# A hybrid decoder layer on one core: the steps of each mixing tile put at other places in the program of the projection and of the feed-forward part

## The chip, the cores and the metric

One core of one Trainium2 chip runs the whole layer in one launch. The metric is device microseconds of a run. The kernel before takes 2847.31 us (median of three runs, 2841.47 to 2847.5). Five engines matter here: TensorE (PE, with its weight loads PEld), VectorE (DVE), ScalarE (ACT), GpSimd (POOL, unused) and SyncE (SP), which issues nearly all DMAs. Each runs its own list of instructions in order; between engines there are only semaphores.

## The reference, cut to what matters

2048 tokens of width 1024 in float32 go through one layer:

```
z   = rms_norm(x) @ w_in                       # 1024 -> 2560
rwkv  = delta-rule recurrence on token-shifted z[:, :1792], 8 heads x 64, then group norm and gate
swa   = windowed softmax attention (128 tokens, sinks, relative bias) on z[:, 1792:], 8 query heads, 2 kv heads
x   = x + concat(rwkv, swa) @ w_out
x   = x + square(relu(rms_norm(x) @ w_ff_up)) @ w_ff_down      # 1024 -> 4096 -> 1024
x   = x + rms_norm(p @ ple_proj) * sigmoid(x @ ple_gate)
out = rms_norm(x)
```

The recurrence is computed in chunks of 64 tokens: decays by a cumulative sum, scores inside a chunk, a triangular inverse built by doubling, and a state of 64x64 per head that is carried from chunk to chunk.

## The kernel before, in words

**Large matrix products.** Tokens come in 4 blocks of 512. Every float32 operand of a large product is split into a rounded part (`hi`, made by ACT) and the rest (`lo`, made by DVE), and three products are added: hi by hi, hi by lo, lo by hi. Weights come in chunks of 128x1024; a chunk is used for 24 matmuls of 128x512. Its `w_hi` is a copy on ACT (line 991), its `w_lo` a subtraction on DVE (line 1312). There are two buffers of each, so chunk n+1 is prepared while PE uses chunk n.

**Two programs side by side.** The work is written as generators that `yield`. The *fill* is the large products: `proj` (projection of a block, lines 583 to 587) or `fin` (output projection, feed-forward, gate: lines 829 to 833 and 871 to 875). Between two yields of the fill PE has, with few exceptions, half a chunk, 12 matmuls; this is called a piece here. The other program is `mix`: the recurrence and the attention of one tile of 128 tokens, 16 tiles in all, each cut into 27 steps (0 to 26). `side_by_side` merges them: a table gives for each step of four tiles a *place*, the number of pieces of the fill that come ahead of it. All engines follow the same table, each with its own part of the step.

- `BESIDE_PROJ`: tiles 0 to 3 beside the projection of blocks 1 to 3 (128 pieces). Pieces 1 to 44 are block 1, 45 to 88 block 2, 89 to 128 block 3. The first 14 of a block's 20 chunks also give DVE the token shift of the projected rows (lines 1356 to 1365) between its two halves.
- `BESIDE_FIN`: tiles 4 to 7 beside `fin` of block 0, and by the same table 8 to 11 and 12 to 15 beside blocks 1 and 2. The fourth `fin` runs alone.

**What the steps do on PE**, and what they wait for:

| step | PE | waits for |
|---|---|---|
| 0 | nothing, but it waits | `rw` of the tile before (DVE, step 25, line 1583) |
| 1 | lora and gate products (640 to 644) | sigmoid of ACT, step 0 (1090) |
| 2 | norms (651) | ACT sigmoids of step 1 (1097) |
| 4 | spread (658) | ACT square root, DVE reciprocal, ACT copy (1101, 1448, 1104) |
| 6 | bonus and transposes (665, 628) | DVE steps 4 and 5 (1459 to 1473) |
| 8, 9 | scores (685), then av and logits (697 to 605) | DVE and ACT copies, DVE masks |
| 10 to 14 | doubling levels (713); probabilities turned (614) at 12; values (622) at 13 | DVE `m` of the level (1514); DVE probabilities (1411) |
| 15, 16 | inverse blocks (728, 735), turn (614) | DVE inverse (1529), DVE copy |
| 17 | values (622), u and w (748, 754) | ACT copy of the turned probabilities (1084), DVE copy |
| 18, 19 | state applied (762), state grown (770, 771), first chunk | DVE copies `wT` (1552), `sa` (1415) |
| 20, 21 | the same, second chunk, and output parts (792, 794) | DVE `state0` (1425), `sa` (1415) |
| 22 | output from the state (802) | itself |
| 25 | output transposed (810) | DVE `y_norm` (1578), after mean and variance in steps 22 to 24 |

Within a step's place nothing of the fill lies between two steps: if steps 18 and 19 have one place, PE waits for the copy between them; if they are one piece apart, it has 12 large matmuls to do in that time. DVE and ACT have the same order: a DVE operation of a step that has to wait holds back the `w_lo` behind it.

Of the kernel before, what the change touches and what calls it, by code (L numbers as in the profile page):

```python
# [161 lines left out]
for _turned, _last in (("turn0", "out1_3"), ("xt0", "ple1_3")):  # L162
# [15 lines left out]
FIN_CHUNKS = 8 + HG * 16 + 2 + 8  # L178


BESIDE_PROJ = (3, 5, 5, 5, 6, 7, 9, 11, 13, 14, 15, 17, 19, 20, 22, 24, 26, 27, 27, 28, 29, 29, 29, 29, 29, 31, 31, 31, 34, 34, 34, 35,
# [3 lines left out]
BESIDE_FIN = (0, 1, 2, 4, 4, 4, 6, 6, 10, 12, 13, 16, 18, 22, 23, 25, 28, 29, 31, 32, 33, 34, 34, 35, 38, 38, 40, 40, 40, 44, 46, 46,  # L185
# [3 lines left out]


def side_by_side(fill, tiles, places):


    assert len(places) == MIX_STEPS * len(tiles)
    given = 0
    for i, place in enumerate(places):
        while given < place:
            next(fill)
            given += 1
        next(tiles[i // MIX_STEPS])  # L200
    for t in tiles:
        assert next(t, None) is None
    for _ in fill:
        pass


def one_after_another(*parts):
    for p in parts:
        yield from p


def whole_program(norm, proj, mix, fin):

    for part in (norm(0), proj(0)):
        for _ in part:
            pass
    side_by_side(one_after_another(proj(1), proj(2), proj(3)), [mix(t) for t in range(TPB)], BESIDE_PROJ)
    for b in range(1, BLOCKS):
        side_by_side(fin(b - 1), [mix(t) for t in range(b * TPB, (b + 1) * TPB)], BESIDE_FIN)
    for _ in fin(BLOCKS - 1):  # L220
# [1559 lines left out]
```

## Time and profile before

| | |
|---|---|
| runs | 2847.31 us median, 2841.47 to 2847.5 (3 runs) |
| profiled execution, span | 2842.6 us; 4.7 us under the median |
| PE busy | 2784.0 us (98%) |
| DVE, ACT busy | 1737.4 us (61%), 1167.5 us (41%) |
| DMA | 317.47 MB, 112 GB/s |
| projection beside tiles 0 to 3 | 134 to 616 us |
| `fin` of blocks 0, 1, 2 beside tiles | 616 to 1200, to 1783, to 2367 us |
| `fin` of block 3 alone | 2367 to 2842.6 us |

The trace gives the span; the times of whole runs include what lies around it. The page puts an operation's idle time in front of it and names what ended the wait. A PE matmul here lasts 0.39 us by the record but the next starts 0.23 us after it, since matmuls overlap; so the distance between starts is what counts, and a stop under 0.16 us isn't seen as idle time.

### The profile page before, as it was taken

What the parts mean: (1) busy time and instruction counts of PE and PEld (TensorE: products, weight loads), DVE (VectorE), ACT (ScalarE), POOL (GpSimd) and SP (SyncE); (2) the same over time, 40 slices, a digit from 0 to 9 for tenths busy, and PEclk for the clock granted to TensorE, in tenths of its full rate; (3) what the DMA queues carried; (4) which work ended last, traced back from release to release, by engine and by line L of the source; (5) the groups of instructions that cost most, each with busy time, mean ns of one, the idle gap of its engine ahead of it and who ended that gap; (6) DMA issues with size and microseconds to landing.
All of it is one profiled execution on the core that took longest, in us unless ns stands there. A gap on an engine that the chain in (4) does not pass through costs nothing.

```text
span 2842.6 us, 54416 instructions
## 1 busy us (share of the span) xinstructions
PE 2784.0 (98%) x23651; PEld 2251.3 (79%) x23651; DVE 1737.4 (61%) x2886; ACT 1167.5 (41%) x1942; POOL 0.2 (0%) x4
## 2 busy tenths in 40 slices
PE   8999999999999999999999999999999999999998
PEld 6877777777878787878887777878887788888876
DVE  5476676756666565675756566766575655443335
ACT  4354344344433342564333334543343335332225
POOL 0000000000000000000000000000000000000000
PEclk9999999999999999999999999999999999999999
DMA  6553443453333232343332333423333225233332
GB/s 211 162 167 97 146 130 97 136 178 98 89 95 95 86 96 93 122 157 91 92 93 85 96 96 130 155 75 92 101 95 87 84 96 185 89 96 97 97 101 77
DMA packets 369738, 317.47 MB, mean 112 GB/s; under 512 B 47291, under 2 KB 322012, under 8 KB 369500
## 3 DMA queue, kind: packets, MB, share of 16 engines
q1 hardware_dynamic: 365104, 309.58, 35.7%
q10 hardware_dynamic: 4396, 4.41, 0.5%
q8 instruction: 187, 3.06, 0.4%
q14 instruction: 51, 0.42, 0.0%
HBM read 276.18 MB, written 39.32 MB: 111 GB/s over the span
## 4 chain that ended last, share of the span: by engine, by line
PE 78%; DVE 2%; DMA 1%; ACT 1%; issue 0%; SPq 0%; ACTq 0%
PE ps L829 13%; PE ps L833 12%; PE ps L832 12%; PE ps L871 9%; PE ps L875 8%; PE ps L874 8%; PE ps L713 1%; PE ps L583 1%; PE ps L586 1%; PE ps L587 1%; PE ps L605 1%; DMA wraw_f<-in_w_gate 1%; PE ps L614 1%; PE ps L622 1%; PE ps L685 1%; PE ps L628 1%
## 5 line engine op out<-in xcount | busy, mean ns | idle before, releaser
L1312 DVE TENSOR_TENSOR w_lo<-wraw_f,w_hi 128x1024 fp32r<-128x1024 f32 x408 | 498.8, 1222 | 405.4 <-ACT w_hi L991 404.5
L991 ACT ACTIVATE w_hi<-wraw_f 128x1024 fp32r<-128x1024 f32 x408 | 430.9, 1056 | 553.4 <-PE ps L829 462.8
L829 PE MATMUL ps<-w_hi,h_hi 128*128 128x512 f32 x1280 | 513.0, 401 | 7.2 <-DVE rw L1583 4.4
L833 PE MATMUL ps<-w_hi,h_lo 128*128 128x512 f32 x1280 | 499.6, 390 | 0.0
L832 PE MATMUL ps<-w_lo,h_hi 128*128 128x512 f32 x1280 | 498.8, 390 | 0.0
L871 PE MATMUL ps<-act_hi,w_hi 128*128 128x512 f32 x1024 | 408.4, 399 | 0.4
L875 PE MATMUL ps<-act_hi,w_lo 128*128 128x512 f32 x1024 | 399.3, 390 | 0.0
L874 PE MATMUL ps<-act_lo,w_hi 128*128 128x512 f32 x1024 | 398.9, 390 | 0.0
L829 PEld LDWEIGHTS ps<-w_hi,h_hi 128*128 128x128 f32 x1280 | 240.3, 188 | 62.8 <-issue 7.9
L833 PEld LDWEIGHTS ps<-w_hi,h_lo 128*128 128x128 f32 x1280 | 240.2, 188 | 52.3
L832 PEld LDWEIGHTS ps<-w_lo,h_hi 128*128 128x128 f32 x1280 | 240.7, 188 | 46.4
L1192 ACT ACTIVATE h_hi<-tmp 128x512 fp32r<-128x512 f32 x128 | 80.9, 632 | 405.7 <-DVE tmp L1634 405.7
L871 PEld LDWEIGHTS ps<-act_hi,w_hi 128*128 128x128 f32 x1024 | 192.2, 188 | 43.5 <-issue 3.7
L875 PEld LDWEIGHTS ps<-act_hi,w_lo 128*128 128x128 f32 x1024 | 192.2, 188 | 41.2
L874 PEld LDWEIGHTS ps<-act_lo,w_hi 128*128 128x128 f32 x1024 | 192.4, 188 | 37.5
L1637 DVE TENSOR_TENSOR h_lo<-tmp,h_hi 128x512 fp32r<-128x512 f32 x128 | 88.7, 693 | 159.5 <-ACT tmp L1193 159.5
L1634 DVE SCALAR_TENSOR_TENSOR tmp<-ps,stage_f 128x512 f32<-128x512 f32 x128 | 88.2, 689 | 117.5 <-PE ps L875 114.8
L583 PE MATMUL ps<-act_hi,w_hi 128*128 128x512 f32 x320 | 129.9, 406 | 5.5 <-DVE rw L1583 2.9
L583 PE MATMUL ps<-h_hi,w_hi 128*128 128x512 f32 x320 | 129.2, 404 | 2.8 <-DVE rw L1583 1.5
L829 PE MATMUL ps<-w_hi,act_hi 128*128 128x512 f32 x320 | 127.4, 398 | 2.7 <-DVE w_lo L1312 2.3
L587 PE MATMUL ps<-act_hi,w_lo 128*128 128x512 f32 x320 | 125.8, 393 | 0.0
L586 PE MATMUL ps<-act_lo,w_hi 128*128 128x512 f32 x320 | 125.8, 393 | 0.0
(231 smaller groups left out, 4078.8 us busy)
## 6 DMA issues: line engine op xcount, KB each, us to landing
wraw_f<-in_w_ff_up SPq DMA_DIRECT2D x256, 256.0 KB, 3.3
wraw_f<-in_w_ff_down SPq DMA_DIRECT2D x128, 512.0 KB, 4.0
wraw_f<-in_w_in SPq DMA_DIRECT2D x80, 512.0 KB, 4.3
zT<-tmp SPq DMA_DIRECT2D x80, 256.0 KB, 2.1
wraw_f<-in_w_out SPq DMA_DIRECT2D x32, 512.0 KB, 4.0
wraw_f<-in_w_gate SPq DMA_DIRECT2D x32, 512.0 KB, 5.1
zs<-zT SPq DMA_DIRECT2D x16, 896.0 KB, 6.6
h_lo<-mixT SPq DMA_DIRECT2D x4, 2048.0 KB, 8.1
```

What stands on the lines that cost most here:

```text
L583: mm = T.matmul(dst, wh, hi[:, k, :], start=(k == 0), stop=False)
L586: T.matmul(dst, wh, lo[:, k, :], start=False, stop=False)
L587: mm = T.matmul(dst, wl, hi[:, k, :], start=False, stop=(k == DK - 1))
L829: mm = T.matmul(ps[:, j, :], ah, wh, start=(first and k == 0), stop=False)
L832: T.matmul(ps[:, j, :], ah, wl, start=False, stop=False)
L833: mm = T.matmul(ps[:, j, :], al, wh, start=False, stop=(final and k == 1))
L871: mm = T.matmul(ps[:, bank, :], wh, act_hi[:, k, :], start=(k == 0), stop=False)
L874: T.matmul(ps[:, bank, :], wh, act_lo[:, k, :], start=False, stop=False)
L875: mm = T.matmul(ps[:, bank, :], wl, act_hi[:, k, :], start=False, stop=(k == DK - 1))
L991: S.activation(w_hi[:, n % 2, :], raw[:, n % 4, :], ACT.Copy).then_inc(w_hi_done, 1)
L1312: V.tensor_tensor(w_lo[:, n % 2, :], raw[:, n % 4, :], w_hi[:, n % 2, :].bitcast(F32), ALU.subtract).then_inc(w_lo_done, 1)
L1637: V.tensor_tensor(h_lo[:, i, :], tmp[:, i % 2, :], h_hi[:, i, :].bitcast(F32), ALU.subtract).then_inc(fin_dve.mark(f"h_lo{g}_{i}"), 1)
```

## The change: other places for the steps, in both tables

Only the numbers of the two tables change. Every instruction is the same, and so is the fill. One line of each table:

```diff
-BESIDE_PROJ = (3, 5, 5, 5, 6, 7, 9, 11, 13, 14, 15, 17, 19, 20, 22, 24, 26, 27, 27, 28, 29, 29, 29, 29, 29, 31, 31, 31, 34, 34, 34, 35,
+BESIDE_PROJ = (11, 14, 15, 19, 21, 24, 26, 26, 30, 34, 35, 37, 39, 40, 42, 43, 45, 46, 47, 48, 50, 52, 52, 55, 55, 59, 61, 61, 62,
...
-BESIDE_FIN = (0, 1, 2, 4, 4, 4, 6, 6, 10, 12, 13, 16, 18, 22, 23, 25, 28, 29, 31, 32, 33, 34, 34, 35, 38, 38, 40, 40, 40, 44, 46, 46,
+BESIDE_FIN = (0, 1, 2, 4, 4, 4, 6, 6, 8, 12, 13, 14, 15, 19, 23, 25, 28, 29, 30, 32, 34, 36, 37, 37, 38, 41, 41, 42, 43, 44, 45, 46,
```

Places of the steps that matter, before and after (tile 0 is the first of a table's four):

| table, tile | steps | before | after |
|---|---|---|---|
| projection, 0 | 0, 1, 2, 4 | 3, 5, 5, 6 | 11, 14, 15, 21 |
| projection, 0 | 17 to 22; 25; next 0 | 27, 27, 28, 29, 29, 29; 31; 31 | 46, 47, 48, 50, 52, 52; 59; 61 |
| projection, 1 | 0, 1, 2, 4, 5 | 31, 34, 34, 35, 35 | 61, 62, 62, 62, 62 |
| projection, 1 | 13, 14, 15, 16 | 49, 50, 53, 54 | 75, 75, 76, 78 |
| projection, 1 | 17 to 22; 25; next 0 | 55, 55, 55, 55, 56, 56; 61; 61 | 78, 78, 78, 78, 78, 78; 81; 81 |
| projection, 2 | 1, 2, 4 | 63, 63, 64 | 83, 83, 84 |
| projection, 2 | 17 to 22; 25; next 0 | 84, 84, 84, 85, 85, 85; 87; 88 | 98, 98, 98, 98, 98, 98; 100; 101 |
| projection, 3 | 0, 1, 2, 4, 5 | 88, 89, 89, 90, 92 | 101, 102, 102, 102, 102 |
| projection, 3 | 13, 14, 15 | 106, 107, 109 | 113, 113, 114 |
| projection, 3 | 17 to 22; 25 | 112, 113, 113, 114, 115, 115; 119 | 117, 117, 117, 117, 117, 117; 119 |
| fin, 0 | 10, 11, 12, 13 | 13, 16, 18, 22 | 13, 14, 15, 19 |
| fin, 2 | 24, 25; tile 3: 0, 1 | 110, 113; 113, 115 | 109, 111; 112, 112 |
| fin, 3 | 24, 25, 26 | 153, 158, 158 | 153, 158, 158 |

Tile 0 beside the projection gets 50 pieces instead of 28, the other three get some 20 each instead of 27 to 31. Beside `fin` every tile keeps about its share.

PE beside the projection, second tile, norms and spread (names: `ones` and `work` into `ps` are the norms, `alpha_t` the spread; `w_hi`, `w_lo` and `act` are the fill). Before:

```order
L641 MATMUL ps<-zs,lora 128x128
L644 MATMUL ps<-zs,gup 128x128 x4
L651 MATMUL ps<-ones,work 128x2 [waits mix_act]
L651 MATMUL ps<-ones,work 128x2 x3
L583 MATMUL ps<-act_hi,w_hi 128x512
L586 MATMUL ps<-act_lo,w_hi 128x512
L587 MATMUL ps<-act_hi,w_lo 128x512
```

The same place after:

```order
L641 MATMUL ps<-zs,lora 128x128
L644 MATMUL ps<-zs,gup 128x128 x4
L651 MATMUL ps<-ones,work 128x2 [waits mix_act]
L651 MATMUL ps<-ones,work 128x2 x3
L658 MATMUL ps<-con,alpha_t 128x128 [waits mix_act]
L658 MATMUL ps<-con,alpha_t 128x128 x3
L583 MATMUL ps<-h_hi,w_hi 128x512 [waits proj_act,w_lo_done]
```

The piece of the fill that lay between norms and spread has gone behind the spread.

DVE beside the projection, third tile, its end (`work<-ps` at 1552 is `wT`, at 1415 `sa`; `state`, then the sums of `y`). Before:

```order
L1552 COPY work<-ps 128x2x4x64 [waits mix_pe]
L1415 COPY work<-ps 64x2x4x64 [waits mix_pe]
L1420 TENSOR_TENSOR small<-ps,state 128x256 [waits mix_pe]
L1425 TENSOR_TENSOR state<-small,ends 128x256 [waits mix_dve]
L1312 TENSOR_TENSOR w_lo<-wraw_f,w_hi 128x1024 [waits w_hi_done]
L1415 COPY work<-ps 64x2x4x64 [waits mix_pe]
L1420 TENSOR_TENSOR small<-ps,state 128x256 [waits mix_pe]
L1425 TENSOR_TENSOR state<-small,ends 128x256 [waits mix_pe,mix_dve]
```

After:

```order
L1552 COPY work<-ps 128x2x4x64 [waits mix_pe]
L1415 COPY work<-ps 64x2x4x64 [waits mix_pe]
L1420 TENSOR_TENSOR small<-ps,state 128x256 [waits mix_pe]
L1425 TENSOR_TENSOR state<-small,ends 128x256 [waits mix_dve]
L1415 COPY work<-ps 64x2x4x64 [waits mix_pe]
L1420 TENSOR_TENSOR small<-ps,state 128x256 [waits mix_pe]
L1425 TENSOR_TENSOR state<-small,ends 128x256 [waits mix_pe,mix_dve]
```

The weight chunk's `w_lo` no longer lies between the two halves; steps 17 to 22 are one run of waits.

PE beside `fin`, end of the third tile (810 is the transposed output, 829 to 833 the fill, `lora` the first product of the fourth tile). Before:

```order
L833 MATMUL ps<-w_hi,h_lo 128x512
L810 MATMUL ps<-con,work 128x128 [waits mix_dve]
L810 MATMUL ps<-con,work 128x128 x3
L829 MATMUL ps<-w_hi,h_hi 128x512 [waits mix_dve]
L832 MATMUL ps<-w_lo,h_hi 128x512
```

After:

```order
L810 MATMUL ps<-con,work 128x128 [waits mix_dve]
L810 MATMUL ps<-con,work 128x128 x3
L829 MATMUL ps<-w_hi,h_hi 128x512
L832 MATMUL ps<-w_lo,h_hi 128x512
...
L833 MATMUL ps<-w_hi,h_lo 128x512
L640 MATMUL ps<-zs,lora 128x128 [waits mix_act,mix_dve]
L641 MATMUL ps<-zs,lora 128x128
```

The wait for `rw` stands one piece later, ahead of the next tile's first product.

## Rows read from the trace of the kernel before

**Rows 1.** Windows by stage; columns: stretch, length, busy by engine, PEclk, DMA.
```profile
134.00:616.00 482.00, 463.62 (x4861) 371.74 (x4860) 330.61 (x648) 204.83 (x358) 0.00 (x0) 0.99 0.45 134
616.00:1200.00 584.00, 577.26 (x5387) 464.68 (x5386) 370.08 (x612) 243.45 (x409) 0.00 (x0) 1.00 0.33 101
```
**Rows 2.** PE's waits, 134 to 616 us: total, times, longest.
```profile
PE ps L583 <- DVE rw L1583: 4.4, 2, 2.9
PE ps L770 <- DVE work L1415: 3.9, 5, 0.8
PE ps L583 <- DVE w_lo L1312: 3.1, 3, 1.4
PE ps L762 <- DVE work L1552: 2.4, 3, 0.8
PE ps L640 <- ACT zs L1090: 1.5, 2, 1.2
PE ps L651 <- ACT work L1097: 1.3, 4, 0.7
PE ps L762 <- DVE state L1425: 1.0, 1, 1.0
```
**Rows 3.** PE's waits, 616 to 2358 us.
```profile
PE ps L829 <- DVE rw L1583: 4.4, 3, 1.5
PE ps L640 <- ACT zs L1090: 3.1, 1, 3.1
PE ps L614 <- DVE work L1411: 2.3, 3, 0.8
```
**Rows 4.** Timeline of PE: start, us, what, idle before.
```profile
253.37 0.63 PE L586 MATMUL ps<-act_lo,w_hi 128*128 128x512 f32 x1
253.80 0.63 PE L587 MATMUL ps<-act_hi,w_lo 128*128 128x512 f32 x1
...
399.94 0.39 PE L586 MATMUL ps<-h_lo,w_hi 128*128 128x512 f32 x1
400.17 0.40 PE L587 MATMUL ps<-h_hi,w_lo 128*128 128x512 f32 x1
...
675.78 1.04 PE L842 MATMUL ps<-con,x 128*128 128x128 f32 x8
```
**Rows 5.** Windows at the two falls of the granted clock.
```profile
248.50:251.90 3.40, 1.38 (x9) 0.93 (x7) 3.27 (x8) 3.35 (x4) 0.00 (x0) 1.00 0.22 73
344.00:351.00 7.00, 6.03 (x48) 4.88 (x44) 2.52 (x6) 0.00 (x0) 0.00 (x0) 0.51 0.01 2
```
**Rows 6.** Timeline, second tile, norms to spread and on.
```profile
264.53 1.05 PE L651 MATMUL ps<-ones,work 128*128 128x2 f32 x8 [0.16 <-ACT work L1097]
265.53 1.28 ACT L1101 ACT_TABLE_LOAD   x1
266.82 0.18 ACT L1101 ACTIVATE knorm<-ps 128x8 f32<-128x8 f32 x1
267.48 0.63 ACT L1104 ACTIVATE alpha_t<-knorm 128x512 f32<-128x512 f32 x1 [0.48 <-DVE knorm L1448]
273.51 0.69 DVE L1473 TENSOR_TENSOR work<-work 128x512 f32<-128x512 f32 x1
```
**Rows 7.** Timeline, second tile, steps 18 to 20 at one place.
```profile
341.98 0.68 PE L762 MATMUL ps<-state,work 64*64 64x64 f32 x16 [0.79 <-DVE work L1552]
345.96 1.12 PE L762 MATMUL ps<-state,work 64*64 64x64 f32 x16 [0.97 <-DVE state L1425]
347.01 0.79 PE L583 MATMUL ps<-h_hi,w_hi 128*128 128x512 f32 x1
```
**Rows 8.** Timeline, second tile, the copy that step 17 waits for.
```profile
335.83 1.03 ACT L1084 ACTIVATE work<-ps 128x1024 f32<-128x1024 f32 x1 [1.04 <-PE ps L614]
```
**Rows 9.** DVE groups by line: busy us, mean ns, idle before.
```profile
L1388 DVE SCALAR_TENSOR_TENSOR work<-ps,bias 128x512 f32<-128x512 f32 x64 | 40.7, 676 | 17.6 <-PE ps L605 17.2
L1396 DVE TENSOR_REDUCE top<-work 128x4 f32<-128x1024 f32 x32 | 39.0, 1220 | 1.1
```

12 rows, old and new, of tables (BESIDE_FIN, BESIDE_PROJ) are left out of this document.

## The prediction

> **What bounds the kernel now.** I read first the windows by stage: beside the projection TensorE (PE) is busy 463.6 of 482 us, beside a block of `fin` 577.3 of 584 [rows 1]. PE is the bound nearly everywhere, its work isn't changed, and other places can only move PE's stops. So next its waits: about 18 us beside the projection [rows 2] and about 10 us beside three blocks of `fin` [rows 3]. That is all there is to win. Third the timeline of PE: a large matmul follows the last by 0.23 us, a piece of twelve takes 12 x 0.228 = 2.73 us; after the longest stop beside the projection, 2.9 us, the same matmuls start 0.43 us apart [rows 2, 4]. Fourth the granted clock: the stretch ahead of the end of that stop had PE busy 1.38 of 3.40 us at full clock, then it fell to half (1.2 GHz); around 344 to 351 us it was at 0.51 [rows 5]. A stop is thus paid twice if the clock falls on it.
>
> Durations are from the profiled execution, whose span of 2842.6 us is 4.7 us under the median of the runs. I sum changes against its span and add them to the median, 2847.3; that gap is itself within the spread of the runs, so 0.2% (5.7 us) is what I count as no change.
>
> **Beside `fin`: what goes.** (a) The tile at places 75 to 113 ends with its transposes at 113, and the next tile's step 0, at 113 too, makes PE wait for `rw`: 4.4 us in three blocks [rows 3]. Now the transposes stand at 111, step 0 at 112, and its wait lands ahead of the lora product, one piece (2.73 us) later: longer than the 1.5 us waited. Nothing is left of it. (b) Level 2 with the turn of the probabilities stood at 18, behind a short piece of transposes, 1.04 us [rows 4], and with VectorE's (DVE's) `out_add` ahead of its DVE part: 2.3 us of waiting in three blocks, 0.8 each [rows 3]. Now it is at 15 behind a full piece of 2.73 us, 1.7 us more cover than before. Gone, but the DVE part of step 12 now comes ahead of the `out_add` that the first transposes wait for; I put 0.3 us a block, bounds 0 and 0.8 (the whole wait come back, by its row). Together with 0.1 us at each restart: -4.4 - 2.3 - 0.4 + 0.9 = **-6.2 us**; bounds -7.1 and -4.7. The first block's 3.1 us for ACT's sigmoid [rows 3] stays, since steps 0 and 1 keep 0 and 1 and the last steps of the table are the same. Everywhere else in this table dependent steps that come closer are one piece apart, as other tiles had them before without a stop.
>
> **Beside the projection: what goes.** Tile 0 gets room. The `rw` wait of 2.9 us at its end goes (25 at 59, next 0 at 61). Steps 0 to 5 go apart, so one `w_lo` wait of 1.4 us (of 3.1 in three) goes with the sigmoid's 0.3 and 0.5 us at the norms; its steps 20 and 21 part (0.8). Tile 3's sigmoid wait of 1.2 us goes, because at 101 ScalarE (ACT) comes to step 0 after preparing a chunk and not after a copy that needs the end of a piece, and so does the `w_lo` wait of 1.3 us behind it [rows 2]. Sum 2.9 + 1.4 + 1.3 + 1.5 + 0.5 + 0.8 = **-8.4 us**; bounds -6 and -9. Tile 1's `rw` wait of 1.5 us stays (25 and 0 both at 81).
>
> **What comes.** Tiles 1 to 3 get 20 pieces each and several dependent steps at one place.
> (c) Steps 2 and 4 at one place, in tiles 1 and 3. From the start of the norms to the end of ACT's copy is 264.53 to 267.48 + 0.63 = 268.11, 3.6 us; PE's own burst in it is 1.05 [rows 6]. The piece that covered this is gone: 2.6 us of waiting, twice, **+5.2**. DVE's part of steps 2 to 5 ends 274.20 - 264.53 = 9.7 us after the norms' start in both orders [rows 6], and the next `w_lo` then has until two pieces and the burst of step 6 are done (about 11.8 us), so no further stop: bounds 0 and 1.4 us a time, the latter the `w_lo` row.
> (d) Steps 17 to 22 at one place in tiles 1, 2 and 3. Each meeting is priced in this trace: 17 to 18 0.8 us, 18 to 19 and 20 to 21 0.8, 19 to 20 1.0 [rows 2, 7]. Before, 3, 5 and 1 of them met (7.4 us); after, 3, 6 and 3 (2.4 + 4.8 + 3.0 = 10.2). One of the 0.8 is counted in tile 0 already, so +2.8 + 0.8 = **+3.6**.
> (e) Tile 1 has step 17 at 78 with 16: ACT's copy of the turned probabilities, 1.03 us [rows 8], lies open, **+1.0**.
> (f) In tiles 1 and 3 steps 13 and 14 share a place and 15 is one piece later. DVE has the logits (2 x 0.68 + 1.22 us [rows 9]) and more ahead of the inverse. An estimate of 0.7 us each, bounds 0 and 2.6 (all of that work open), **+1.4**.
> (g) Tile 2 ends in a zone where DVE has the token shift, steps 22, 25, 0 at 98, 100, 101: 0.8 us for `y_norm` and `rw`, and 0.2 for the masks at 88: **+1.0**, bounds 0 and 2.9 (the `rw` wait of tile 0, which lay in such a zone).
> Without the clock the projection part is -8.4 + 5.2 + 3.6 + 1.0 + 1.4 + 1.0 = **+3.8 us**.
>
> **The clock.** Before it fell twice. After the 2.9 us stop a piece ran at 0.43 for 0.23 us [rows 4]: 12 x 0.20 = 2.4 us. In the run of steps 17 to 20 of tile 1 the second state product took 1.12 for 0.68 us [rows 7], and nine large matmuls after it 0.2 us more each: about 2.5 with the small ones. So 4.9 us were lost. After, the first cause is gone, but steps 17 to 22 make three runs that are each longer than that one. I take one fall in each: 3 x 2.5 = 7.5, **+2.6 us**. Bounds: none (-4.9) and five, with the two waits of (c) (+7.6). For (c) the row of the 2.9 us wait speaks for a fall, that of the 3.1 us wait at the start of `fin` against: there the stage ran at 1.00 [rows 1, 3].
>
> The Trainium skill, "TensorE: Matmul & The Clock Gate", section "HAM oscillation — how this bites in real kernels", says that waits which break up the stream of matmuls let the gate fall back to half rate, and that each later burst then starts cold. The half-rate matmuls after the 2.9 us wait agree [rows 4]; the 3.1 us wait didn't bring one. This is the rule that speaks most against the change, and it is weighed as the rival "slower" below.
>
> Sum: -6.2 + 3.8 + 2.6 = +0.2 us. Forecast **2848 us**, no change that can be told.
>
> **Rivals.** *Faster, 2837 us:* the three dense runs keep full clock, as the denser half of tile 2's end did before (17 to 19 at one place, no fall), and the estimates of (f) and (g) don't come: +0.2 - 7.5 - 2.4 = -9.7. For it: three of four tile ends of before had no fall inside them. Against: the one that had four steps at one place had it.
> *Slower, 2855 us:* the spread wait of (c) is where it is decided. DVE has 9.7 us of work in one place while the token shift of the fill waits behind it; if its `w_lo` comes late, PE stops again, 1.3 us twice, and the two waits together pull the clock down, 2.5 us twice: +0.2 + 7.6 = +7.8. It decides from the point where the clock falls at both. For it: such waits for `w_lo` followed the dense starts of tiles 0 and 3 [rows 2]. Against: the sum in (c), and the other `rw` wait, 1.5 us, brought no fall.
> *The waits beside `fin` only change their name, 2852 us:* the fourth tile's steps 0 and 1 now share place 112, and PE may wait there for the sigmoid, up to the 1.2 us of the projection [rows 2], three times: +0.2 + 3.6 = +3.8. Against it: the second tile had 40 and 40 there before and didn't stop.
> *Table switches of ACT cost twice in the open, 2850 us.* In the uncovered chain of (c) a table load stands, 1.28 us, and the square root starts at once behind it [rows 6]; if ACT held each of the two chains for that length once more, it is +2.6. Against it is the same row, which has nothing between load and square root.
> The Trainium skill, "ScalarE: Activation LUTs", section "What ACT_TABLE_LOAD costs", gives 1283 ns for the load and 1380 ns more for a drain at each switch. By it the chain in (c) would be 1.38 us longer each time, 2.8 us in all. The row has the load's 1.28 us and no drain behind it [rows 6], so the trace doesn't agree.
>
> **How the numbers follow.** Forecast 0.48, faster 0.20, slower 0.22, renamed waits 0.06, table switches 0.04. The forecast's own spread, from the bounds of (f), (g) and one fall more or less, is 2842 to 2854, a little of it beyond 0.2% on each side (0.03 faster, 0.04 slower). Faster: 0.19 of the faster case plus 0.03, 0.22; slower: 0.20 of the slower case plus 0.04, 0.24; the rest, 0.54, is no change. The range runs to both main rivals, 2837 to 2857; beyond it lie the cases in which all bounds fall to one side.
>
> **What would show it.** PE's waits beside `fin` for `rw` and for the probabilities are gone (6.7 us to under 1). Beside the projection PE waits for ACT's `alpha_t` copy ahead of line 658 twice, some 2.6 us each; six waits at line 770 and three for `state`; no wait of 2.9 us for `rw`. The granted clock falls three times, at the ends of tiles 1, 2 and 3. Stage by stage: projection +6 us, each `fin` block -2. The prediction is wrong if the clock falls not at all or five times, or if `w_lo` heads the waits beside the projection.

## The result: slower by 0.44%, and the profile after

The changed kernel takes 2856.22 us (median of five runs, 2854.35 to 2858.99), the kernel before 2842.13 us beside it; the ratio is 1.0044, 95% interval 1.0031 to 1.0057. That is slower by 12.5 us by the ratio, more than the 0.2% that I counted as no change. The time lies at the upper end of the range; the likeliest case, no change, didn't come true, and the rival "slower, 2855 us" did.

That the time lies so near to that rival's is in part luck. The prediction counted from 2847.3 us, the median of the first three runs of the kernel before; with two more runs that median is 2842.13. So the rival's change was +7.8 us and the range ended at +9.7 us, while the measured change is +12.5 us (8.8 to 16.2 by the interval): larger than either.

The page after, its first line and part 1 (busy us, share, instructions):

```profile
span 2854.2 us, 54416 instructions
PE 2794.3 (98%) x23651; PEld 2260.1 (79%) x23651; DVE 1740.3 (61%) x2886; ACT 1166.4 (41%) x1942; POOL 0.2 (0%) x4
```

The span is 11.6 us longer. The windows of the changed kernel, cut at the same matmul of the fill in each kernel (stretch, length, busy time by engine, PEclk, DMA): the projection beside tiles 0 to 3, its block 3 alone, and `fin` of block 1:

```profile
134.37:626.55 492.18, 469.05 (x4862) 379.40 (x4861) 331.57 (x648) 204.85 (x357) 0.00 (x0) 0.97 0.44 131
448.07:626.55 178.48, 167.74 (x2005) 135.52 (x2004) 118.68 (x232) 62.83 (x113) 0.00 (x0) 0.93 0.42 125
1214.71:1797.78 583.07, 580.76 (x5402) 466.84 (x5401) 379.21 (x628) 247.48 (x421) 0.00 (x0) 1.00 0.34 104
```

The same cuts in the kernel before:

```profile
133.48:615.76 482.28, 463.90 (x4862) 371.97 (x4861) 330.61 (x648) 205.12 (x357) 0.00 (x0) 0.99 0.45 134
1203.02:1786.87 583.85, 580.33 (x5401) 467.34 (x5400) 378.53 (x628) 247.66 (x421) 0.00 (x0) 1.00 0.34 104
```

The projection is 9.9 us longer; the two full `fin` blocks are 0.8 and 0.9 us shorter. The rest of the 11.6 us: 0.9 us more ahead of the projection and 1.6 us in `fin` 3, whose programs are as before, and 0.9 us in `fin` 0. Each of the three has a stretch at half clock (6.8, 3.4 and 3.4 us) that the trace of the kernel before has not. PE's waits beside the projection (total, times, longest), against [rows 2]:

```profile
PE ps L658 <- ACT alpha_t L1104: 5.3, 2, 2.8
PE ps L770 <- DVE work L1415: 4.8, 6, 0.8
PE ps L762 <- DVE state L1425: 2.9, 3, 1.0
PE ps L583 <- DVE w_lo L1312: 2.6, 2, 2.0
PE ps L762 <- DVE work L1552: 2.4, 3, 0.8
PE ps L728 <- DVE work L1529: 1.5, 2, 0.8
PE ps L553 <- DVE rw L1583: 1.5, 1, 1.5
PE ps L622 <- ACT work L1084: 1.2, 1, 1.2
```

All of PE's waits there add up to 22.9 us instead of 18.1 (the windows above give 23.1 and 18.4). Beside `fin`, against [rows 3]:

```profile
PE ps L640 <- ACT zs L1090: 3.1, 1, 3.1
PE ps L829 <- DVE w_lo L1312: 2.3, 3, 0.8
PE ps L829 <- DVE act_lo L1643: 1.8, 3, 0.6
PE ps L871 <- DVE w_lo L1312: 1.4, 3, 0.5
PE ps L842 <- DVE act_lo L1622: 0.8, 3, 0.3
```

The waits for `rw` and for the probabilities are gone, and three smaller ones stand there, the last three rows (the first two rows were there before). Now the clock. It was at half beside the projection in five stretches, four of them below (the fifth, 3.4 us, from 336 us on):

```profile
401.00:407.70 6.70, 4.92 (x90) 4.55 (x88) 1.97 (x4) 0.00 (x0) 0.00 (x0) 0.50 0.05 9
493.20:499.90 6.70, 5.98 (x116) 5.79 (x120) 1.04 (x2) 0.00 (x0) 0.00 (x0) 0.50 0.26 41
517.10:523.80 6.70, 5.10 (x14) 4.22 (x15) 6.15 (x16) 5.25 (x9) 0.00 (x0) 0.50 0.26 78
585.30:595.50 10.20, 8.37 (x148) 7.80 (x148) 1.97 (x4) 0.00 (x0) 0.00 (x0) 0.50 0.17 27
```

401, 493 and 585 us are the ends of tiles 1, 2 and 3 (steps 17 to 22 at one place); 336 and 517 us are the two waits of the spread. 34.1 us at half clock in all, against 13.7 before. The first wait of the spread, on PE's timeline, against [rows 6]:

```profile
332.55 1.05 PE L651 MATMUL ps<-ones,work 128*128 128x2 f32 x8 [0.15 <-ACT work L1097]
336.17 1.12 PE L658 MATMUL ps<-con,alpha_t 128*128 128x128 f32 x4 [2.57 <-ACT alpha_t L1104]
```

From the start of the norms to the spread is 3.62 us, as it was when a piece lay over it, and the spread itself ran at half clock (1.12 us for four transposes that take 0.60 at full).

This is one execution of each kernel, and the clock isn't the same in every one. e2 and e7 below have the old table beside the projection, so this stage is the same program in them as in the kernel before. Their windows, e2 first:

```profile
133.74:613.46 479.72, 461.36 (x4863) 370.12 (x4861) 330.61 (x648) 204.88 (x357) 0.00 (x0) 0.99 0.46 135
133.84:612.46 478.62, 460.12 (x4862) 368.98 (x4861) 330.64 (x648) 204.90 (x357) 0.00 (x0) 1.00 0.46 135
```

PE stands idle 18.4 and 18.5 us in them, as before, but the half clock lasts 6.8 and 3.4 us instead of 13.7, and the stage is 2.6 and 3.7 us shorter: about 0.37 us for each us at half clock. The new program of the stage (the changed kernel and e1) ran twice too, with 34.1 and 41.0 us at half clock, in 492.2 and 497.2 us. So some us of a stage's length belong to the execution and not to the table.

### The profile page after: what moved, and what is told of

Read it like the earlier page. It is cut to its first block, busy times and chain, and to the rows that moved or that the text cites. A ratio compares the mean times of both kernels' runs of the same rounds, so it can differ in the third digit from the quotient of the medians.

```text
span 2854.2 us, 54416 instructions
## 1 busy us (share of the span) xinstructions
PE 2794.3 (98%) x23651; PEld 2260.1 (79%) x23651; DVE 1740.3 (61%) x2886; ACT 1166.4 (41%) x1942; POOL 0.2 (0%) x4
## 4 chain that ended last, share of the span: by engine, by line
PE 76%; DVE 3%; ACT 2%; DMA 1%; issue 1%; SPq 0%; ACTq 0%
PE ps L829 12%; PE ps L833 12%; PE ps L832 12%; PE ps L871 9%; PE ps L875 8%; PE ps L874 8%; PE ps L713 1%; PE ps L605 1%; DMA wraw_f<-in_w_gate 1%; PE ps L622 1%; PE ps L583 1%; PE ps L614 1%; PE ps L586 1%; PE ps L587 1%; PE ps L685 1%; PE ps L770 1%
## 5 line engine op out<-in xcount | busy, mean ns | idle before, releaser
L875 PE MATMUL ps<-act_hi,w_lo 128*128 128x512 f32 x1024 | 399.2, 390 | 0.0
L874 PE MATMUL ps<-act_lo,w_hi 128*128 128x512 f32 x1024 | 399.0, 390 | 0.0
L586 PE MATMUL ps<-h_lo,w_hi 128*128 128x512 f32 x320 | 125.9, 393 | 0.0
L587 PE MATMUL ps<-h_hi,w_lo 128*128 128x512 f32 x320 | 125.8, 393 | 0.0
```

The source lines that it names most:

```text
L586: T.matmul(dst, wh, lo[:, k, :], start=False, stop=False)
L587: mm = T.matmul(dst, wl, hi[:, k, :], start=False, stop=(k == DK - 1))
L874: T.matmul(ps[:, bank, :], wh, act_lo[:, k, :], start=False, stop=False)
L875: mm = T.matmul(ps[:, bank, :], wl, act_hi[:, k, :], start=False, stop=(k == DK - 1))
```

## Experiments

Four readings were open at first. **A**: the loss is made beside the projection, by steps that meet at one place and by the falls of the clock that these meetings bring. Rivals: **B**, the `fin` table has a good part in it; **C**, the waits count and the falls cost next to nothing; **D**, VectorE is behind in the dense tiles whatever the order, so that a wait taken away turns up as another. In the kernels e1 to e4 the lines stand 6 lower than in the listing (line 652 is 658 there), in e6 6 to 10 higher, since the tables or the code ahead have another length.

### e1 and e2: one table each

```diff
 e1: the new BESIDE_PROJ, the old BESIDE_FIN
 e2: the old BESIDE_PROJ, the new BESIDE_FIN
```

> The new table beside the projection alone, the old one beside fin. Theory A (the loss is made beside the projection, by steps that meet at one place and by the falls of the clock that this brings): the projection stage is 10 us longer than before, as in the changed kernel, the fin blocks as before; about 2852 to 2855 us, ratio 1.004. Rival B (the fin table has a good part in it): 2845 us, ratio 1.001.

Measured 2859.5 us, ratio 1.0055 (1.0041 to 1.0069): more than A had. In the trace the projection stage is 14.9 us longer than before and not 10, with 41.0 us at half clock and 24.7 us of idle time.

> The new table beside fin alone, the old one beside the projection. Theory A: 0.8 us less in each of three blocks, 2840 us, ratio 0.999; the waits for rw and for the probabilities are gone, and new ones of 0.5 us for w_lo, 0.3 us for act_lo and 0.6 us for the split of p stand in their place. My prediction's own size for it was 2 us a block, 2836 us. Rival B: slower than before, 2846 us or more.

Measured 2844.39 us, ratio 0.9997 (0.9988 to 1.0005); `fin` of blocks 1 and 2 583.2 and 583.5 us. All of the loss comes with the table beside the projection. B falls. By the trace the `fin` table is worth 0.7 us a block, a third of what I had put; the whole times can't show so little.

### e3 and e5: the spread behind a piece again

```diff
 e3: tiles 1 and 3 beside the projection, steps 2, 4, 5, 6
-62, 62, 62, 64 and 102, 102, 102, 104
+62, 63, 63, 64 and 102, 103, 103, 104
```

> The changed kernel with steps 4 and 5 one piece later in tiles 1 and 3 beside the projection (62 to 63, 102 to 103), nothing else. Theory A: the two waits of 2.6 and 2.7 us at line 658 go, and with them the two falls of the clock there: 8 to 10 us less than the changed kernel, about 2847 us. Rival C (waits alone count, the falls cost next to nothing): 5 us less, 2851 us. Rival D (VectorE is behind there anyway, so the wait moves to w_lo): within 1 us of the changed kernel.

Measured 2863.81 us, ratio 1.0070 (1.0057 to 1.0083): slower than the changed kernel, which none of the three had. PE's waits beside the projection in e3 (first two):

```profile
PE ps L659 <- DVE work L1464: 10.8, 2, 5.5
PE ps L764 <- DVE work L1409: 4.7, 6, 0.8
```

The waits of 2.6 us are gone, and line 659 (665 in the listing, step 6) waits 5.4 us twice for step 5. The first of the two, on the timelines of ScalarE and VectorE:

```profile
339.82 1.04 ACT L985 ACTIVATE w_hi<-wraw_f 128x1024 fp32r<-128x1024 f32 x1
340.89 1.22 DVE L1306 TENSOR_TENSOR w_lo<-wraw_f,w_hi 128x1024 fp32r<-128x1024 f32 x1 [2.85 <-ACT w_hi L985]
344.56 1.13 DVE L1464 SCALAR_TENSOR_TENSOR work<-work,par,zs 128x128 f32<-128x128 f32 x4
```

With the piece between steps 2 and 4, the next `w_lo` stands ahead of step 5 on VectorE. It needs `w_hi`, and ScalarE starts that only at 339.82 us, behind a table load and three activations of the tile (2.9 us). So VectorE stands idle for 2.85 us, a time in which it began step 5 in the changed kernel, and then `w_lo` and 3.7 us of step 5 follow, with one piece on PE to cover them. It is the same at tile 3, 2.85 us again. I had moved the wait one step on and made it larger. So e5 moved what hangs on it too:

```diff
 e5: the same tiles, steps 4 to 9
-62, 62, 64, 64, 66, 68 and 102, 102, 104, 105, 106, 107
+63, 63, 65, 65, 67, 69 and 103, 103, 105, 106, 107, 108
```

> The changed kernel with steps 4 and 5 one piece later in tiles 1 and 3 beside the projection, and now steps 6 to 9 too (63, 63, 65, 65, 67, 69 and 103, 103, 105, 106, 107, 108), so that VectorE has two pieces for step 5 as in the kernel before. Theory A: no wait at line 658 and none at 665; the two falls of the clock at the spread go; 2847 to 2850 us. Rival D (VectorE is behind in these places whatever the order): waits of 2 us or more at 665 or for w_lo stay, 2854 us or more.

Measured 2858.38 us, ratio 1.0058 (1.0045 to 1.0070), not told apart from the changed kernel's. Three of its waits:

```profile
PE ps L583 <- DVE w_lo L1312: 6.9, 4, 2.7
PE ps L685 <- DVE kappa_t L1488: 1.4, 1, 1.4
PE ps L665 <- DVE work L1470: 1.3, 2, 0.7
```

The falls at the spreads didn't come (23.9 us at half clock), but the idle time grew to 25.4 us, with `w_lo` at its head. What D foretold came: the wait turned up elsewhere, and the time is over 2854 us. But D's reason, VectorE's own amount of work, isn't what the trace shows. Here too VectorE stands idle 2.85 us ahead of that `w_lo`, until ScalarE has done its share of the tile's start and then `w_hi`; PE waits 1.7 us for this `w_lo` in tile 1 and 1.8 us in tile 3. So the tile's start is held by the chain of ScalarE's tile work, `w_hi` and `w_lo`. Whether a `w_hi` put ahead of that tile work would cure it was not tried.

### e4: one piece inside the tile's end

```diff
 e4: steps 16, 17 to 19, 20 to 22 of tiles 1, 2, 3 beside the projection
-78, 78, 78; 97, 98, 98; 116, 117, 117
+78, 78, 79; 96, 97, 98; 115, 116, 117
```

> The changed kernel with one piece of the fill put between steps 19 and 20 of tiles 1, 2 and 3 beside the projection, nothing else but what this pushes (tile 2 and 3 have steps 16 to 19 one piece earlier, tile 1 steps 20 to 24 one later). Theory A: the three waits of 1.0 us at line 762 for the state go, and the runs of small matmuls are short enough that the clock falls in at most one of the three: 3 us by the waits and 4 to 7 us by the clock, about 2847 us. Rival C (waits alone): 3 us less, 2853 us, with the falls in place or without cost.

Measured 2850.15 us, ratio 1.0027 (1.0016 to 1.0038): 4.8 us less than the changed kernel by the two ratios. The time lies between the forecasts of A (2847) and C (2853), and the intervals of the two ratios overlap, so the trace has to decide. The waits for the state are gone, while the wait for `sa` (line 764, 770 in the listing) grew in one place:

```profile
PE ps L764 <- DVE work L1409: 6.3, 6, 2.4
PE ps L652 <- ACT alpha_t L1098: 5.3, 2, 2.8
```

Idle time as a whole is even 0.8 us more (23.7 for 22.9), so the waits explain none of the gain. Time at half clock fell from 34.1 to 17.1 us, and the projection stage is 2.8 us shorter in spite of the idle time: some 3.6 us for 17.0, 0.2 us for each us at half clock. This speaks for A and against C. A's count was off, though: the clock still fell in four of the five places, two of them tile ends (1 and 3), for 3.4 us each time, and once more for 3.4 us at 160 us.

### e6: the waits kept, and filled

```diff
+def busy(n, tiles=(2, 3)):
+    if t in tiles:
+        for _ in range(n):
+            T.matmul(ps[:, 3, :], act_hi[:, 0, 0:P], act_hi[:, 0, :], start=True, stop=True)
 # behind the norms of tile 3: busy(11); behind steps 17, 18, 19, 20 of tiles 2 and 3: busy(4) each
```

> The changed kernel with matmuls that nobody reads (128x512, 0.23 us each, into a bank that is free in block 3 of the projection) in the waits of tiles 2 and 3: eleven behind the norms of tile 3, four behind each of steps 17, 18, 19 and 20 of tiles 2 and 3. The waits keep their length and are filled. Theory A (half of the loss is the clock): the three falls at 493, 517 and 585 us don't come, 24 us at half clock are gone, and it is 6 to 9 us faster than the changed kernel, 2847 to 2850 us, though it does more work. Rival C (only the waits cost): within 1 us of the changed kernel, or up to 1 us slower by the fillers that outlast a wait.

Measured 2853.27 us, ratio 1.0038 (1.0025 to 1.0051). The windows of e6: block 3 of the projection, and the three places where the clock had fallen:

```profile
451.31:623.25 171.94, 170.54 (x2048) 135.02 (x2047) 118.56 (x232) 62.85 (x113) 0.00 (x0) 1.00 0.44 130
480.00:500.00 20.00, 20.00 (x292) 15.60 (x292) 10.95 (x22) 3.56 (x5) 0.00 (x0) 1.00 0.33 100
500.00:530.00 30.00, 29.42 (x210) 23.44 (x207) 24.95 (x55) 19.43 (x31) 0.00 (x0) 1.00 0.33 90
575.00:600.00 25.00, 24.94 (x367) 20.04 (x362) 13.08 (x25) 5.89 (x8) 0.00 (x0) 1.00 0.29 75
```

With 43 more matmuls block 3 took 171.94 us instead of 178.48: 6.5 us less, at full clock all through. The waits were as long as before (the norms of tile 3 to its spread 3.80 us, for 3.82); only the 23.9 us at half clock are gone. That gives 6.5 / 23.9 = 0.27 us lost for each us at half clock, 1.9 us for a fall of 6.8 us. C falls for this block. The whole gained less than its block, 1.7 us by the ratios, where A had 6 to 9, and the intervals overlap: the whole times alone wouldn't decide. In this execution the blocks ahead, which have no fillers, took 3.4 us more than in the changed kernel's: the fall at tile 1 lasted 10.2 us instead of 6.8, and there was one more of 3.4 us at 160 us.

### e7, e9 and e10: what the fin table gives and takes

```diff
 e7: the kernel before, fin, tile 0: steps 11, 12; tile 2: steps 24, 25, 26
-16, 18; 110, 113, 113
+14, 15; 110, 111, 112
 e9:  as e2, tile 0 step 13:  19 -> 22
 e10: as e2, tile 3 steps 3 to 10:  117, 123, 125, 128, 129, 133, 136, 136 -> 117, 120, 123, 125, 125, 128, 133, 134
```

> The kernel before with only two places of the fin table changed in kind: tile 0 steps 11 and 12 at 14 and 15 (was 16, 18), tile 2 steps 25 and 26 at 111 (was 113). Theory E (the new fin table cures the two waits of 0.8 and 1.5 us a block and pays it back by three new ones that come from its other changes): without those, 2.3 to 2.5 us a block, 7 us in all, ratio 0.9975, 2836 us. Rival F (the two waits come back elsewhere whatever the rest does): 2841 us or more.

Measured 2839.66 us, ratio 0.9987 (0.9978 to 0.9996). By the traces `fin` 1 is 581.96 us, 1.9 us less than before, and so are the others; 5.8 us in three blocks, of which the medians show 3.7. That is between E (2836 us) and F (2841 us or more); the blocks speak for E, whose 2.3 to 2.5 us a block were somewhat too many. (Step 26 of tile 2 stood at 112, not at 111.) Its waits beside `fin` are these, without the first block's for the sigmoid:

```profile
PE ps L829 <- DVE w_lo L1312: 2.3, 3, 0.8
PE ps L842 <- DVE act_lo L1622: 0.8, 3, 0.3
```

> The fin-only kernel (old table beside the projection, new one beside fin) with step 13 of tile 0 back at 22 (was 19). Read from the waits, since the times are too close. Theory E: the wait of 0.5 us for w_lo at line 871 at the first chunk of the feed-forward part goes in all three blocks, since VectorE no longer has the second logits (4.4 us) ahead of that w_lo; the 0.3 us for act_lo at 842 stays, as it comes from steps 11 and 12 being early. Rival: both stay or both go.

> The fin-only kernel with steps 3 to 10 of tile 3 back at 117 to 134. Theory E: the wait of 0.6 us at line 829 for act_lo of line 1643 (the split of p, piece 133) falls back to the 0.1 us of before, since the four masks of step 8 (2.7 us of VectorE) no longer stand at 133 ahead of it; the others stay. Rival: 0.5 us or more stays.

Both were run once (2842.95 and 2843.07 us); only their waits are read. e9:

```profile
PE ps L829 <- DVE w_lo L1312: 2.4, 3, 0.8
PE ps L829 <- DVE act_lo L1643: 1.8, 3, 0.6
PE ps L842 <- DVE act_lo L1622: 0.8, 3, 0.3
```

and e10:

```profile
PE ps L829 <- DVE w_lo L1312: 2.3, 3, 0.8
PE ps L871 <- DVE w_lo L1312: 1.4, 3, 0.5
PE ps L842 <- DVE act_lo L1622: 0.8, 3, 0.3
```

Each took away the wait that was named and left the other. The three new waits have three causes: step 13 (VectorE's logits ahead of a `w_lo`), step 8 of tile 3 (its masks ahead of the split of p; e10 moved steps 4 to 10 together), and, as the wait that e7, e9 and e10 all keep, steps 11 and 12 (ahead of the `out_add`). No run undid the last one alone.

### e11: the meeting of norms and spread alone, in the roomy table

```diff
 e11: the kernel before, tiles 1 and 3 beside the projection, steps 2, 4, 5
-34, 35, 35 and 89, 90, 92
+34, 34, 34 and 89, 89, 89
```

> The kernel before with steps 4 and 5 put at the place of step 2 in tiles 1 and 3 beside the projection (34 and 89), nothing else. It prices the uncovered spread by itself in the roomy table. Theory A: two waits of 2.6 us at line 658, and a fall of the clock at each in some runs, 2 us a fall: 5 to 9 us slower than before, ratio 1.002 to 1.003. Rival D (VectorE has the same work there in any order, so a wait at 658 is only a wait taken early): the w_lo wait of 1.3 us in tile 3 goes and less than 4 us are lost, ratio 1.0015 or less.

Measured 2849.29 us, ratio 1.0020 (1.0011 to 1.0029), 5.7 us. Three of its waits:

```profile
PE ps L658 <- ACT alpha_t L1104: 5.2, 2, 2.6
PE ps L651 <- ACT work L1097: 1.8, 4, 1.3
PE ps L583 <- DVE w_lo L1312: 0.4, 1, 0.4
```

Of the 5.2 us, 2.7 came back from `w_lo` (3.1 before), so idle time grew by 2.8 us only; the clock fell at both spreads, 6.8 us each. This execution also had a fall of 6.8 us at 151 us, where the kernel before had none, and it is 3.1 us above the median of its kernel. The median's 5.7 us lies in A's range of 5 to 9 and over D's 4. Both theories are in it: D for half of the wait, A for the falls.

### e8 and e12: a version that beats both

```diff
 e8: fin as e7; beside the projection the old table, and
 tile 1: step 0 31 -> 32; steps 17 to 22  55,55,55,55,56,56 -> 55,55,56,57,58,58
 tile 2: step 0 61 -> 62; steps 15 to 22  81,83,84,84,84,85,85,85 -> 81,82,83,84,85,86,86,86
 tile 3: step 0 88 -> 89; steps 1, 2, 4  89,89,90 -> 91,91,92; steps 18 to 22  113,113,114,115,115 -> 113,114,115,116,116
 ... (a few steps beside these are a piece or two later too)
```

> The same fin table, and beside the projection the table of before with its own meetings parted: step 0 of tiles 1, 2 and 3 one piece later, so that the rw waits have a piece over them; steps 18 to 21 of tiles 1, 2 and 3 one piece apart. Theory A: the rw waits of 2.9 and 1.5 us, the meetings of steps 18 to 20 (4 us of the waits) and the two falls of the clock go: 8 to 12 us less than with the fin table alone, about 2826 us, ratio 0.994. Rival D (VectorE is behind and the waits turn up at w_lo): 2834 us or more.

Measured 2835.67 us, ratio 0.9975 (0.9966 to 0.9984): the fastest, 0.7% below the changed kernel. Its projection:

```profile
133.96:608.90 474.94, 459.77 (x4862) 367.24 (x4861) 330.47 (x648) 205.00 (x357) 0.00 (x0) 1.00 0.46 136
```

7.3 us less than before with 3.2 us less idle time, and not one fall beside the projection. But e7, which has the old table there, took 478.62 us with one fall of 3.4 us. Against it the new places are worth 3.7 us, 3.3 of them idle time, and the medians of e7 and e8 differ by 4.0 us. That is less than half of the 8 to 12 us forecast, and the time is what rival D had (2834 us or more): waits turned up at 651, 685 and 810 (1.4, 1.4, 1.3 us), and those for `w_lo` grew from 3.1 to 4.0 us.

> The kernel with both tables mended, mended further: steps 1 to 7 of tile 1 a piece later, tile 2 with step 16 at 83 and 24, 25 at 88, 89, tile 3 with steps 0 to 12 a piece or two later. Theory A: the waits at 651 (1.4 us), 810 (1.3), 614 (1.0) and 685 (1.4) go, 3 to 5 us, ratio 0.996, 2832 us. Rival D (VectorE is behind): they turn up as waits for w_lo and the ratio stays at 0.9975.

```diff
 e12: e8 with tile 1 steps 1 to 7 at 35,35,35,36,36,38,38; tile 2 steps 16, 24, 25 at 83, 88, 89;
 tile 3 steps 0 to 12 at 91,92,92,92,93,94,96,96,99,100,101,103,105
```

Measured 2838.09 us, ratio 0.9980 (0.9971 to 0.9989), no better. The waits that it was made for shrank or went, and a larger one came, the first line below (e8 has 4.0 us in the second):

```profile
PE ps L665 <- DVE work L1470: 4.5, 1, 4.5
PE ps L583 <- DVE w_lo L1312: 3.6, 4, 1.7
```

It is the mistake of e3 again, in tile 1: its steps 4 and 5 are a piece later, a `w_lo` has come ahead of step 5, and VectorE stands idle 2.85 us for its `w_hi`. Idle time beside the projection is that of e8 (15.1 us for 15.2); the stage is 3.2 us longer, with 10.2 us at half clock for none.

## Why the prediction came out as it did, step by step

- **The waits beside the projection were nearly right.** I had +3.8 us; idle time grew 4.8. Two waits at 658 (5.2 forecast, 5.3 measured), six at 770, three for the state, one of 1.2 at 622, two of 0.75 at 728: each came. Two of its terms were off. Of the -8.4 us, 2.7 stood for two `w_lo` waits; that row fell by only 0.5 us. Tile 0 starts later, but a wait of 0.6 and one of 2.0 us for `w_lo` stood behind pieces 6 and 8, ahead of its first step; the second is at the same chunk as the 1.4 us of before. There ACT had sat idle for the weight's DMA (5.4 us ahead of `w_hi`), so the chunk came late without the steps too. And (g) brought 0.2 us, not 1.0.
- **The clock is the step that failed.** By the prediction's own sign, "wrong if the clock falls not at all or five times", its mechanism was wrong: it took one fall in each of the three tile ends, +2.6 us, and held the two spread waits for undecided, with the first `fin` wait against them. The clock fell in all five places; time at half clock rose by 20.5 us, and the stage lost 5.1 us beyond its idle time. The price of a fall was too high (2.5 us; e6 has 1.9 for 6.8 us), the count too low. And the 4.9 us that this term starts from were one execution's: the same program had 3.4 to 13.7 us at half clock in the traces of before, e2 and e7.
- **The `fin` table was mis-sized.** -6.2 us was forecast, and the two waits did go; measured were -0.8 and -0.9 in the blocks that ran at full clock, about -2.5 for three. The 0.3 us that I had for steps 11 and 12 came out at 0.27. e7, with little but the two moves of (a) and (b), gained 5.8 us in the traces, so those terms were near. What failed here is the sentence that the other steps that come closer are one piece apart, as others were before without a stop: it looked at PE's own chain. Steps 13 and 8 had moved VectorE's work in front of a `w_lo` and of the split of p, and PE waits there for the fill (e9, e10).
- **The rival "slower" had the right place and half of the right mechanism.** It was decided at the spread, as it said, and the clock fell at both. The second half, `w_lo` late behind it, didn't show in the changed kernel, since VectorE worked on while PE stood. In e11 the spread wait took over half of its 5.2 us from `w_lo` waits, and in e5, with the piece back, `w_lo` waits took its place: the two are in large part one debt, and ScalarE's `w_hi` is in it. Its +7.8 us was also short of the +12.5 measured.
- The waits beside `fin` didn't just change their name at place 112: no wait at 640 but the first block's. And the table switch of ACT cost nothing more in the open: the norms to the spread took 3.62 us for 3.6.

Open: why the 3.1 us wait at the start of `fin` brought a fall in some traces (the changed kernel, e1, e2, e3, e5, e8, e12) and none in the others (before, e4, e6, e7, e9, e10, e11). Its length is about the same in all. e9 and e10 have the program of e2 there, so the table doesn't decide it alone.

## What to carry to other kernels

Before two dependent steps are put at one place, count both: the wait itself, and whether the tensor engine may lose its clock there, which cost 0.2 to 0.4 us more for each us at half rate where waits lay in the stretch, and nearly 0.5 us where large matmuls stood back to back. A table of places has to be read on the engine that is waited for: moving a step moves that engine's work in front of other deadlines, and parting two steps helps only if what then comes between them is ready: here it was a `w_lo` whose `w_hi` another engine still owed. One execution of a kernel is too few to judge a gain of some us: the kernel before had half clock for 13.7 us in its trace and, with the same places, for 3.4 us in e7. Where a wait can't be removed, useful or even unread matmuls in it can keep the clock, as in e6.

## What the runs showed of the hardware that I had not expected

- A stretch with the same instructions and the same waits may run with or without a fall. The fourth `fin`, whose program none of the kernels changes, took 471.6 us in before, e2, e6, e11 and e12 and 473.2 in the changed kernel, e1, e7 and e8, with 3.4 us at half clock near the same matmuls. The fall follows a wait of 2.5 us that the kernel before has too, and lies on large matmuls back to back: 1.6 us for 3.4 us at half clock, 0.47 for each.
- The mean clock orders the runs of one kernel: the five of the changed one had 2854.4 and 2854.5 us at 0.992, 2856.2 and 2857.6 at 0.990, 2859.0 at 0.989. 0.003 less is 17 us more at half clock (2 x 0.003 x 2857), and 4.6 us in time; with the rounding of the clock that is 0.2 to 0.4 us for each us at half clock, and 0.27 lies in it.
- Small matmuls lose their clock without long stops. At the end of tile 2 no single wait was over 1.0 us (four waits of 0.8 to 1.0 us in 6 us); the clock fell there all the same, and with fillers in the four waits it didn't.
